# Prompt attention of one layer: the compressed weights are transposed in the scores' PSUM bank, and three unused 256-column products are issued per unit

## The reference

```python
s_c = jnp.einsum('bcgqd,bngd->bcgqn', q, kc).astype(jnp.float32) * scale
p_c = masked_softmax(s_c, (dist_c >= 0)[None, :, None, None, :])
o_c = jnp.einsum('bcgqn,bngd->bcgqd', p_c.astype(vc.dtype), vc)
...
p_s = masked_softmax(s_s, (dist_s >= 0)[:, :, :, None, :])
o_s = jnp.einsum('bcgqk,bcgkd->bcgqd', p_s.astype(v_sel.dtype), v_sel)
...
p_w = masked_softmax(s_w, mask_w[None, :, None, None, :])
o_w = jnp.einsum('bcgqw,bwgd->bcgqd', p_w.astype(vw.dtype), vw)
o = g[..., 0:1] * o_c + g[..., 1:2] * o_s + g[..., 2:3] * o_w
```

## Time and profile before

| | |
|---|---|
| time, median of 3 runs | 1970.05 us (1966.56 to 1972.72) |
| the profiled execution's own time | 1973.5 us |
| its span, first to last instruction | 1971.7 us |
| TensorE matmul busy, share of the span | 92% |
| VectorE, ScalarE, GpSimdE busy | 43%, 27%, 35% |
| mean granted clock of TensorE | 0.93 |
| the block of the change | 214.8 to 380.9 us of the span |

### The profile page before, as it was taken

One profiled execution on the slowest core, in us unless ns is written; L12 is line 12 of the kernel. 1 busy time (PEld: TensorE's weight loads), 2 busy tenths in 40 slices (PEclk: granted clock), 3 DMA queues, 4 the chain that ended last, 5 costly groups with the idle time before them and its releaser, 6 DMA issues. The chain is left out here.

```text
span 1971.7 us, 36246 instructions
## 1 busy us (share of the span) xinstructions
PE 1809.8 (92%) x15772; PEld 1725.7 (88%) x15772; DVE 856.0 (43%) x1676; ACT 524.4 (27%) x899; POOL 681.5 (35%) x266
## 2 busy tenths in 40 slices
PE   6998789666895799989999999999999999999997
PEld 5997678544893699789999999999999999999997
DVE  4423466333366444456552055443245555205521
ACT  5112344221224122233221122232213222112211
POOL 2200000000230200045555356565556555436541
PEclk8968787687997899989999999999999999999999
DMA  5530410141320010022222222232222222232222
GB/s 150 115 47 22 140 34 23 33 144 43 92 65 14 17 41 4 5 85 65 86 81 79 91 93 71 62 105 86 86 86 78 73 86 75 81 102 65 78 81 73
DMA packets 158382, 140.89 MB, mean 71 GB/s; under 512 B 17204, under 2 KB 153944, under 8 KB 157840
## 3 DMA queue, kind: packets, MB, share of 16 engines
q1 hardware_dynamic: 158224, 138.58, 23.7%
HBM read 132.67 MB, written 10.02 MB: 72 GB/s over the span
## 5 line engine op out<-in xcount | busy, mean ns | idle before, releaser
L270 POOL TENSOR_TENSOR w_lo<-w_raw,w_hi 128x2048 fp32r<-128x2048 f32 (+2 forms) x109 | 460.1, 4222 | 934.3 <-ACT w_hi L264 934.1
L309 PE MATMUL ps<-h_hi,w_hi 128*128 128x288 f32 x2016 | 433.6, 296 | 0.0
L309 PE MATMUL ps<-h_lo,w_hi 128*128 128x288 f32 x2016 | 433.1, 296 | 0.0
L309 PE MATMUL ps<-h_hi,w_lo 128*128 128x288 f32 x2016 | 432.8, 296 | 0.0
L264 ACT ACTIVATE w_hi<-w_raw 128x2048 fp32r<-128x2048 f32 (+2 forms) x109 | 190.0, 1743 | 504.0 <-PE ps L309 461.4
L309 PEld LDWEIGHTS ps<-h_hi,w_hi 128*128 128x128 f32 x2016 | 323.7, 189 | 0.3
L309 PEld LDWEIGHTS ps<-h_lo,w_hi 128*128 128x128 f32 x2016 | 323.7, 189 | 0.0
L309 PEld LDWEIGHTS ps<-h_hi,w_lo 128*128 128x128 f32 x2016 | 323.5, 189 | 0.0
L418 DVE TENSOR_TENSOR xT<-ps,xT 128x576 f32<-128x576 f32 x48 | 35.6, 756 | 267.0 <-PE ps L309 267.0
L309 PE MATMUL ps<-g_hi,w_hi 128*128 128x288 f32 x704 | 151.0, 295 | 0.0
L309 PE MATMUL ps<-g_lo,w_hi 128*128 128x288 f32 x704 | 151.0, 295 | 0.0
(11 more groups left out here) (493 smaller groups left out, 2879.2 us busy)
## 6 DMA issues: line engine op xcount, KB each, us to landing
w_raw<-in_ffn_up SPq DMA_DIRECT2D x44, 1024.0 KB, 5.1
w_raw<-in_w_in_even SPq DMA_DIRECT2D x12, 1024.0 KB, 6.2
w_raw<-in_ffn_down SPq DMA_DIRECT2D x16, 768.0 KB, 4.9
w_raw<-in_w_in_odd SPq DMA_DIRECT2D x12, 1024.0 KB, 5.2
w_raw<-in_ffn_down SPq DMA_DIRECT2D x16, 640.0 KB, 4.4
BT<-rv SPq DMA_DIRECT2D x8, 520.0 KB, 3.5
seg<-in_cache_cmp_kv SPq DMA_DIRECT2D x32, 128.0 KB
kv_rows<-in_cache_slc_kv SPq DMA_DIRECT2D x32, 128.0 KB, 2.1
```

The source lines that it names most:

```text
L270: pool.tensor_tensor(slab_view(wlo[slot], st), slab_view(raw[slot], st), slab_view(whi[slot], st).bitcast(F32), ALU.subtract).then_inc(w_l ...
L309: last = pe.matmul(ps[:, bank + 2 * j + half, 0:HT], w[slot][:, c:c + 128], x[:, xs + t, half * HT:(half + 1) * HT], start=(t == 0 and n = ...
```

## The change

The transposed compressed weights go to columns 256 to 383 of bank 4 in place of bank 7. Their transpose no longer waits for `o_taken`; it waits for `s_taken` of unit u + 1, whose compressed scores bank 4 holds. The 32-column scores of unit u + 2, which also go to bank 4, wait for a new semaphore `ptc_act` that ScalarE raises when it has copied the transposed weights. The wait for `o_taken` stands behind the scores now, and behind it three products of 256 columns are issued into bank 7, columns 256 to 511, whose results nobody reads. Nothing else changes.

```diff
@@ -1514,8 +1514,9 @@
             den = r.take("den", [128, 2, 3])
             bt_in, s_ready, s_taken, p_ready, pt_ready, pt_act, pt_dve, o_ready, o_taken, m_ready = (sem(x) for x in (
                 "bt_in", "s_ready", "s_taken", "p_ready", "pt_ready", "pt_act", "pt_dve", "o_ready", "o_taken", "m_ready"))
-            on_t, on_ev = sem("on_t"), sem("on_ev")
+            on_t, on_ev, ptc_act = sem("on_t"), sem("on_ev"), sem("ptc_act")
             U = 4 * NH
+            FILL = 3
             with nc.Block() as block:
                 @block.sync
                 def _(sp):
@@ -1543,9 +1544,11 @@
                             pe.wait_ge(s_taken, u)
                         q = q_st[g][:, hh, 128 * qt:128 * qt + 128]
                         nk = 128 * (qt + 1)
-                        for out, keys in ((ps[:, s, 0:nk], [k_mv[0][part][g][:, 0:nk] for part in range(2)]),
-                                          (ps[:, 2 + s, 0:nk], [k_mv[1][part][g][:, 0:nk] for part in range(2)]),
-                                          (ps[:, 4, 0:32], [kc_mv[part][g][:, :] for part in range(2)])):
+                        for n, (out, keys) in enumerate(((ps[:, s, 0:nk], [k_mv[0][part][g][:, 0:nk] for part in range(2)]),
+                                                         (ps[:, 2 + s, 0:nk], [k_mv[1][part][g][:, 0:nk] for part in range(2)]),
+                                                         (ps[:, 4, 0:32], [kc_mv[part][g][:, :] for part in range(2)]))):
+                            if n == 2 and u >= 2:
+                                pe.wait_ge(ptc_act, u - 1)
                             pe.matmul(out, q, keys[0], start=True, stop=False)
                             last = pe.matmul(out, q, keys[1], start=False, stop=True)
                         last.then_inc(s_ready, 1)
@@ -1561,11 +1564,15 @@
                         for kt in range(qt + 1):
                             pe.transpose(ps[:, 5, 128 * kt:128 * kt + 128], sS[s][:, 128 * kt:128 * kt + 128], ident[:, :])
                             pe.transpose(ps[:, 6, 128 * kt:128 * kt + 128], sW[s][:, 128 * kt:128 * kt + 128], ident[:, :])
+                        if u + 2 <= U:
+                            pe.wait_ge(s_taken, u + 2)
+                        pe.transpose(ps[0:32, 4, 256:384], sC[s][:, :], ident[:, :]).then_inc(pt_ready, 1)
+                        if u + 2 < U:
+                            scores(u + 2)
                         if u >= 1:
                             pe.wait_ge(o_taken, u)
-                        pe.transpose(ps[0:32, 7, 256:384], sC[s][:, :], ident[:, :]).then_inc(pt_ready, 1)
-                        if u + 2 < U:
-                            scores(u + 2)
+                        for _ in range(FILL):
+                            pe.matmul(ps[:, 7, 256:512], q_st[g][:, u // 4 % 4, 128 * qt:128 * qt + 128], k_mv[0][0][g][:, 0:256], start=True, stop=True)
                         pe.wait_ge(pt_act, u + 1)
                         pe.wait_ge(pt_dve, u + 1)
                         O = ps[:, 7, 0:192]
@@ -1637,7 +1644,7 @@
                         act.wait_ge(pt_ready, u + 1)
                         if u >= 1:
                             act.wait_ge(o_ready, u)
-                        act.copy(PTc[:, :], ps[0:32, 7, 256:384])
+                        act.copy(PTc[:, :], ps[0:32, 4, 256:384]).then_inc(ptc_act, 1)
                         act.copy(PTs[:, 0:qt + 1, :], ps[:, 5, 0:128 * (qt + 1)].rearrange("p (a b) -> p a b", b=128)).then_inc(pt_act, 1)
                         if u + 1 < U:
                             exps(u + 1)
```

## The result

The changed kernel takes 1944.85 us in the median of four executions (1940.22 to 1946.49), the kernel before 1969.74 us in four of its own. The ratio is 0.987, with a 95% interval of 0.9847 to 0.9893: 1.3% faster, some 25 us. The profiled execution took 1944.15 us with a span of 1942.3.

The account below looks back on a forecast made before the run. Bound: TensorE alone at the low clock, the TensorE-VectorE hand-over at the high one. Start +0.4, units -31.4, end -1.8, flip -2.5 sum to -35.3 us: 1973.5 to 1938.2, or 1935 for the median; range 1929 to 1947.

Parts of the forecast that it names:

- the rival in which the clock still falls: In the block: clock mostly high but falling now and then, 10.9 us per low head, total 1946 to 1957; chance 0.16.
- The four waits of a head ahead of L1566 go: Compressed transpose no longer waits for VectorE's reads of O; 3.1 of 3.7 us of waits per high-clock head go.
- The head at the high clock, 14.2 us: Four units at 2.4 GHz take 14.2 us in place of 15.92, TensorE becoming the bound; ends 13.7 and 15.92.
- The wait on `ptc_act`: 32-column scores wait for ScalarE's copy of the transposed weights: some 0.15 us in one unit of four.
- The first head: First four units of the block, a third of them at the low-clock price: 18.0 us.
- The third bias table: Its load, queued behind eight stores, lands about a microsecond too late for the faster block: 1 us added.
- The clock up to the end of the block: Granted clock high from somewhere in the first head to the block's end; this forecast had chance 0.73, spanning 1930 to 1943.
- Even without the fillers it is further from a fall than now: High-clock heads: with 3 of 3.7 us of waits gone, the clock is less likely to drop, fillers or not.
- moves up whole: Everything behind the block starts anew at a barrier with its own loads, so it only shifts earlier, its time unchanged.
- The profiled one lies 3.45 above the median: Whole kernel: profiled execution 3.45 us over the median, so 1938.2 for such an execution became 1935 for the median.
- x = 3.0 low heads: Old kernel's block: 3.0 of 7.75 heads at the low clock, costing 23 us over the high clock.
- The low state holds itself: Rival, in the block: fillers lengthen already full low-clock units; 1988 us with 5 low heads, 2018 all low; chance 0.05.

Follow-up runs that it names:

- experiments 1 and 2: Changed kernel without its three unused products per unit (move alone): 1954.93 us; changed kernel with the compressed transpose waiting for `o_taken` again, three products kept: 1966.12 us.
- experiments 8 to 10: Changed kernel plus fourteen unused products at the start: 1949.32 us; that with two fillers, eight products before the flip: 1944.55; the first with key/value DMAs queued later: 1940.55.
- Experiment 4: The kernel before, unchanged, run for a second trace: 1969.51 us, block 149.0 us against 159.3 in the first trace.

## Why the prediction was right, and where it was off

The forecast, 1935 us with a range of 1929 to 1947, had the direction and the range right; the gain was 25 us and not 35. By its own working a clock that stays high gives 1930 to 1943, and the range went on to 1947 only for the rival in which the clock still falls. The median lies in that last part, and the rival is not why. Of the mechanism, the waits went and the clock stayed high, as forecast; but it is the fillers that keep it high (experiments 1 and 2), and to the waits I had given a share of that. By its steps:

- The four waits of a head ahead of L1566 go: right, 12.4 us in the block became 0.3.
- The head at the high clock, 14.2 us: measured 14.45. A filler costs 0.18 us in place of 0.12 in the place where it stands; the six-filler kernel gives 0.108 for each further one. The move alone gives 13.91. The work of a head without fillers I had put at 12.3 us; counted back from the full TensorE with six fillers it is about 15.75 - 24 x 0.108 = 13.2, and the 0.5 us that I had added for waits hid most of that. So 14.2 came near partly by luck. Units 4 to 31 took 97.1 us, and by my terms (6.75 x 14.2 + 1) 96.9: this too is luck, since the 1 us for the third bias table was not spent and made up for heads that were too short.
- The wait on `ptc_act`: 0.1 us, foreseen 0.15.
- The first head: 17.6 us, foreseen 18.0; the start 0.6 us late, foreseen 0.4. The latter says nothing: the first copy stands at 222.2 us in one trace of the changed kernel and at 228.6 in the other.
- The third bias table: not waited for in the changed kernel. The mechanism was real, though, and it was waited for as soon as the first head was 3.3 us shorter (experiments 8 to 10).
- The clock up to the end of the block: right, apart from 3.4 us at the flip, which took 6.1 us from the last read of O to its last copy and not 4.5: +1.6.
- "Even without the fillers it is further from a fall than now": not borne out. Without them 47.8 us of the block were low, against 82.4 and 52.0 in the two traces of the kernel before, and 30.7 of these lay in two falls behind the first head. The kernel with the old waits and three fillers had none. That the waits are "the ones that end in a fall" was the part of the reasoning that failed.
- Everything behind the block "moves up whole": the step of the sum that failed first. Behind the block the changed kernel's trace takes 1595.1 us and the earlier one 1590.7, +4.4, with 133 us low in place of 125. The second pair has 1591.3 and 1591.0. So nothing points to an effect of the change; the low stretches behind the block fall differently from execution to execution. Nobody can read that from one trace, and I gave it no width.
- "The profiled one lies 3.45 above the median": carried over to the changed kernel, whose profiled execution lay 0.7 below its own. That is 4.2 us. Experiment 4 points to its source, without proving it: the kernel before had a long block in the trace that I read, 159.3 us, and 149.0 in another. By its term the change wins 34.3 us in the one pair of blocks and 25.6 in the other, and the median over executions, 25, is like the second.

In sum, 1.6 for the flip, 4.4 behind the block and 4.2 from trace to median are the 10 us that were missing. The low share of the kernel before was the term that I mis-sized: I took x = 3.0 low heads from one execution. With the second trace it is (137.6 - 123.4) / 7.7 = 1.8.

Of the rivals, none came, in either of the two traces of the changed kernel. "The low state holds itself" was wrong: with fillers the clock rose in every trace, with the old wait too. What stays open is what the chip asks for: 64 columns did as well as 256, and one filler nearly as well as three, so these runs don't tell the products' length from their number.

## What to carry to other kernels

Where one engine hands a unit to another and gets it back, look for a false dependence by place: here a result shared a PSUM bank with the output that the other engine was still reading, and moving it to another bank took out the wait. Where TensorE's clock changes within a stage, read the granted clock beside each wait, test the waits and the filling apart (here the move took out waits and the fillers held the clock), and price a stage from more than one execution, since the low stretches differ between them. And ask of each speedup what it will now arrive too early for: with the same 14 products the block took 126.6 us in a trace with a queued DMA ahead of the bias table, and 120.1 once the queue was cleared.

## What the runs showed of the hardware that was not expected

A busy TensorE stayed at 0.50 for 37.5 us in the kernel before (35.99 us busy), while the changed kernel, equally full, kept 1.00 for 112.7 us. The trace of the kernel with fourteen more products lost the clock for 6.7 us behind a wait of TensorE of only 1.42 us, and the move alone lost it at 311.6 us behind one of 0.46 us; with fillers it stayed at 1.00 for 131.3 us through 28 waits of up to 0.9 us. So the length of a wait alone does not tell whether the clock falls. Useless products can pay: with the waits gone, 96 of them took the block from 134.6 us to between 123.4 and 125.0 in the traces, at a price of 0.03 us per head for the first of a unit and 0.35 for the third.
